# Up-projection jobs over two and four token quarters, a ring of eight value tiles, and softmax denominators as columns

## The reference

```
cq, ckv, kr, z = split(h @ w_in)                       # 384, 256, 32, 1024 columns
q  = rmsnorm(cq, q_norm) @ w_uq                         # 16 heads x (64 nope + 32 rope)
kv = rmsnorm(ckv, kv_norm) @ w_ukv                      # 16 heads x (64 key + 64 value)
q_rope, k_rope = rope(q[..., 64:], pos), rope(kr, pos)
s  = (q_nope @ k_nope.T + q_rope @ k_rope.T) * scale    # causal
o  = softmax(s) @ v
y  = (o * silu(z)) @ w_out
```

## Time and profile before

| | |
|---|---|
| median of 3 runs | 3116.81 us (3113.44 to 3117.73) |
| profiled execution | 3119.66 us |
| its span | 3117.8 us |
| mean granted TensorE clock | 0.977 |
| DMA over the span | 541.14 MB, 173 GB/s |

### The profile page before, as it was taken

The page is one execution under the profiler, slowest core; times in us unless marked ns, Lnnn a source line. Parts: engine busy times, 40 slices in busy tenths (PEclk is TensorE's granted clock), DMA queues, the critical chain, the costliest instruction groups (busy, mean ns, idle before and its releaser), DMA issues. The chain is left out here.

```text
span 3117.8 us, 41010 instructions
## 1 busy us (share of the span) xinstructions
PE 2946.5 (95%) x13537; PEld 2317.2 (74%) x13537; DVE 1909.3 (61%) x2696; ACT 1628.0 (52%) x2830; POOL 1450.3 (47%) x1163
## 2 busy tenths in 40 slices
PE   7999987998999999999987799999999999899998
PEld 6888885666888787778765477777777777588876
DVE  3543315552588765555653587787887877358875
ACT  3111114766445544444544277777777777544543
POOL 0022104764233440000753388888888888523343
PEclk9999998999999999999999699999999999999999
DMA  5233447665996765554999634434435433498674
GB/s 163 84 131 121 118 126 229 190 207 173 301 273 223 237 211 182 171 163 154 325 357 346 160 72 92 109 74 100 101 72 109 92 72 104 120 300 275 224 236 146
DMA packets 294279, 541.14 MB, mean 174 GB/s; under 512 B 29952, under 2 KB 117632, under 8 KB 286912
## 3 DMA queue, kind: packets, MB, share of 16 engines
q1 hardware_dynamic: 219840, 391.23, 42.6%
q10 hardware_dynamic: 74240, 147.49, 15.4%
HBM read 357.86 MB, written 180.49 MB: 173 GB/s over the span
## 5 line engine op out<-in xcount | busy, mean ns | idle before, releaser
L2528 POOL TENSOR_TENSOR mla_pl<-mla_p,mla_ph 128x512 fp32r<-128x512 f32 (+3 forms) x640 | 707.3, 1120 | 164.0 <-ACT mla_p L2388 156.4
L1479 PE MATMUL end_bank<-end_xh,end_whi 128*128 128x512 f32 x1808 | 717.7, 397 | 45.7 <-DVE end_wlo L1710 17.8
L1481 PE MATMUL end_bank<-end_xh,end_wlo 128*128 128x512 f32 x1808 | 708.1, 392 | 0.0
L1480 PE MATMUL end_bank<-end_xl,end_whi 128*128 128x512 f32 x1808 | 707.9, 392 | 0.0
L1548 ACT CAST end_whi<-early_wraw 128x1024 fp32r<-128x1024 f32 (+1 forms) x228 | 234.0, 1027 | 579.7 <-PE end_bank L1481 520.4
L2387 ACT ACTIVATE mla_ph<-mla_score 128x512 fp32r<-128x512 f32 (+3 forms) x640 | 341.3, 533 | 244.8 <-PE mla_score L2230 239.4
L1710 DVE TENSOR_TENSOR end_wlo<-early_wraw,end_whi 128x1024 fp32r<-128x1024 f32 x188 | 258.2, 1374 | 322.6 <-ACT end_whi L1548 322.2
L1479 PEld LDWEIGHTS end_bank<-end_xh,end_whi 128*128 128x128 f32 x1808 | 342.0, 189 | 135.7 <-DVE end_wlo L1710 25.2
L2411 DVE TENSOR_REDUCE mla_mx<-mla_mx 128x1 f32<-128x512 f32 (+3 forms) x640 | 371.8, 604 | 92.6 <-PE mla_mx L2230 91.9
L2461 DVE TENSOR_TENSOR mla_acc<-mla_acc,mla_p 128x512 f32<-128x512 f32 (+3 forms) x576 | 349.1, 606 | 118.3 <-ACT mla_p L2388 114.4
L1480 PEld LDWEIGHTS end_bank<-end_xl,end_whi 128*128 128x128 f32 x1808 | 342.2, 189 | 72.7 <-issue 2.9
(11 more groups left out here) (235 smaller groups left out, 4983.4 us busy)
## 6 DMA issues: line engine op xcount, KB each, us to landing
early_wraw<-in_pe_gate ACTq DMA_DIRECT2D x64, 512.0 KB, 5.1
early_wraw<-in_w_out ACTq DMA_DIRECT2D x62, 512.0 KB, 7.6
early_wraw<-in_w_in ACTq DMA_DIRECT2D x56, 512.0 KB, 3.8
scratch_q<-in_rope SPq DMA_DIRECT2D x64, 256.0 KB, 2.9
swa_q<-scratch_q SPq DMA_DIRECT2D x8, 2048.0 KB, 9.5
end_factor<-scratch_inv SPq DMA_DIRECT2D x64, 256.0 KB, 9.9
scratch_proj<-end_out_f SPq DMA_DIRECT2D x64, 256.0 KB, 6.8
scratch_sum<-end_out_f SPq DMA_DIRECT2D x64, 256.0 KB, 6.2
```

The lines of the kernel that those rows point to most:

```text
L1479: nc.tensor.matmul(bank, wh[:, at], xh[:, k0 + k, :], start=(k == 0), stop=False)
L1480: nc.tensor.matmul(bank, wh[:, at], xl[:, k0 + k, :], start=False, stop=False)
L1481: last = nc.tensor.matmul(bank, wl[:, at], xh[:, k0 + k, :], start=False, stop=(k == kc - 1))
L2528: pool.tensor_tensor(p_lo[b][:, off:TC], prob[b][:, off:TC], p_hi[b][:, off:TC].bitcast(F32), ALU.subtract).then_inc(p_lo_ok, 1)
```

## The change

The four "uq" jobs become two, each of two quarters, and the four "ukv" jobs become one over all four, so that each weight block is loaded, cast and split once for two quarters (uq) and once in all (ukv). In uq the tiles of a block pair run for the first quarter and then for the second; pairs 1 and 4, and 2 and 5, are interleaved, so that both slots are in use together. The slices of a set are ordered k first, then quarter. A weight split is now placed where both the block before has begun and the block before last has ended. Cosine and sine of the second quarter go to the two free slices of the job's raw set. In ukv all key tiles come before all value tiles. Value tiles go to a ring of eight places in both raw sets instead of three. In the attention, `denominator` makes the four times 128 sums the weights and one column of ones the moving side, so that a chunk's denominators land as four columns; ACT copies these into a 128x256 tile, and at the end of the phase two transposes, two copies and one store replace the 64 row stores. The window attention keeps its rows.

```diff
-            jobs += [(stage, q) for stage in ("in", "uq", "ukv") for q in range(NTC)]
+            jobs += [("in", q) for q in range(NTC)] + [("uq", 0), ("uq", 2), ("ukv", 0)]
+        quarters = dict(uq=2, ukv=NTC)
...
-                for pair in (0, 3, 1, 4, 2, 5):
-                    b = new_block(stage, pair, 2, 2 * Q_LORA)
...
+                for mates in ((0,), (3,), (1, 4), (2, 5)):
+                    mine = [new_block(stage, pair, 2, 2 * Q_LORA) for pair in mates]
+                    for t in (q, q + 1):
+                        for b, pair in zip(mine, mates):
+                            tiles += pair_tiles(b, pair, t)
...
-                    tiles += [dict(job=j, kind="split", i=4 * g + i, q=q, block=b, at=i) for i in range(4)]
+                    tiles += [dict(job=j, kind="split", i=4 * g + i, q=t, block=b, at=i)
+                              for t in range(NTC) for i in range(4)]
...
-                    tiles += [dict(job=j, kind="v", i=h, q=q, block=b, at=i) for i in range(4)]
+                    tiles += [dict(job=j, kind="v", i=h, q=t, block=b, at=i) for t in range(NTC) for i in range(4)]
...
-        block_end = [b["at"] for b in blocks[1:]] + [total]
+        for n, x in enumerate(tiles):
+            blocks[x["block"]].setdefault("at", n)
+            blocks[x["block"]]["end"] = n + 1
...
+        split_at = {}
+        for b in range(n_w, len(blocks)):
+            split_at.setdefault(max(blocks[b - 1]["at"], blocks[b - n_w]["end"]), []).append(b)
...
-            turn_cos, turn_sin = square[0], square[1]
+            def tables_of(n):
+                x = tiles[n]
+                spare = raw[x["job"] % 2]
+                return (square[0][:], square[1][:]) if x["q"] % 2 == 0 else (spare[:, 6, :], spare[:, 7, :])
...
+        n_vals = 8
+        v_stored = [s.sem(f"v_stored{b}") for b in range(n_vals)]
...
         def v_tile(n):
-            m = (values[n] - 1) % 3
-            return raw[tiles[n]["job"] % 2][:, 2 + 2 * m:4 + 2 * m, :].rearrange(
+            m = (values[n] - 1) % n_vals
+            mine = raw[(tiles[n]["job"] - (m < n_vals // 2)) % 2]
+            m %= n_vals // 2
+            return mine[:, 2 * m:2 * m + 2, :].rearrange(
...
-            eng.wait_ge(x_lo, pieces_upto[tiles[n]["job"] - 2])
-            if m >= 3:
-                wait_v_stored(eng, v_tiles[m - 3])
+            eng.wait_ge(x_lo, pieces_upto[tiles[n]["job"]])
+            eng.wait_ge(dve_out, by_dve[turn_tiles[-1]])
+            if m >= n_vals:
+                wait_v_stored(eng, v_tiles[m - n_vals])
...
                 if latent and n == total - 4:
-                    for m in range(first[-2], first[-2] + 8):
+                    for m in range(first[-2] + 24, first[-2] + 32):
                         wait_stored(sp, m)
...
+                if nq > 1 and n == first[j]:
+                    pe.wait_ge(x_lo, pieces_upto[j])
...
             def denominator(c):
...
-                mm(o_ps[c % 2][:], consts["ones"][:], acc[c % 2][:], True, True).then_inc(den_ok, 1)
+                for j in range(TC // P):
+                    last = mm(o_ps[c % 2][:, j:j + 1], acc[c % 2][:, j * P:(j + 1) * P], consts["ones"][:, 0:1], True, True)
+                last.then_inc(den_ok, 1)
+
+            def turn_denominators():
+                pe.wait_ge(row_ok, len(chunks))
+                for b in range(n_den // P):
+                    op = nc.tensor.transpose(score[b][:, 0:P], den_cols[:, b * P:(b + 1) * P], consts["ident"][:])
+                op.then_inc(den_turned, 1)
...
+                    per = TC // P
+                    act.copy(den_cols[:, per * c:per * (c + 1)], o_ps[c % 2][:, 0:per]).then_inc(row_ok, 1)
...
+            def store_denominators():
+                act.wait_ge(den_turned, 1)
+                for b in range(n_den // P):
+                    op = act.copy(den_t[:, b, :], score[b][:, 0:P])
+                op.then_inc(den_copied, 1)
+                act.wait_ge(den_copied, 1)
+                act.dma_start(cfg["dens_dst"], den_t[:]).then_inc(dens_stored, 16)
```

More of the change, by code:

```diff
@@ L1071, in chain_phase, with chunks @@
         if latent:
-            jobs += [(stage, q) for stage in ("in", "uq", "ukv") for q in range(NTC)]
+            jobs += [("in", q) for q in range(NTC)] + [("uq", 0), ("uq", 2), ("ukv", 0)]
+        quarters = dict(uq=2, ukv=NTC)
         depth = dict(proj=KD, wo=KD, pe=KD, uq=Q_LORA // P, ukv=KV_LORA // P)
         depth["in"] = KD
+        def chunks(stage):
+            return depth[stage] * quarters.get(stage, 1)
         tiles, first, blocks = [], [], []
         def new_block(stage, i, loads, width):
-            blocks.append(dict(stage=stage, i=i, at=len(tiles), loads=loads, width=width))
+            blocks.append(dict(stage=stage, i=i, loads=loads, width=width))
             return len(blocks) - 1
@@ L1151, in row_ends @@
             return n == mates[0], n == mates[-1]
-        n_pieces = [-(-depth[stage] // 2) for stage, _ in jobs]
+        n_pieces = [-(-chunks(stage) // 2) for stage, _ in jobs]
         pieces = [(j, p) for j in range(len(jobs)) for p in range(n_pieces[j])]
@@ L1164, in part_of, with quarter_of @@
             j, p = pieces[n]
-            return slice(2 * p, min(2 * p + 2, depth[jobs[j][0]]))
+            return slice(2 * p, min(2 * p + 2, chunks(jobs[j][0])))
+        def quarter_of(j, c):
+            stage, q = jobs[j]
+            return q + c % quarters.get(stage, 1)
         def slot_of(j, part):
@@ L1452, in _ @@
                     sp.wait_ge(turn_stored[b], 16 * len(turn_tiles))
[L1453 to L1454 removed]
+                for b in range(n_vals):
+                    sp.wait_ge(v_stored[b], 16 * sum((values[n] - 1) % n_vals == b for n in v_tiles))
         @block.tensor
@@ L1466, in tile @@
                 k0, kc = (2 * x["q"], 2) if kind == "proj" else (0, depth[jobs[j][0]])
+                nq = quarters.get(jobs[j][0], 1)
+                if nq > 1:
+                    k0 = x["q"] - jobs[j][1]
+                if nq > 1 and n == first[j]:
+                    pe.wait_ge(x_lo, pieces_upto[j])
                 wh, wl = w_hi[b % n_w], w_lo[b % n_w]
@@ L1545, in split_w @@
                 if b >= n_w:
-                    act.wait_ge(product, block_end[b - n_w])
+                    act.wait_ge(product, blocks[b - n_w]["end"])
                 width = blocks[b]["width"]
@@ L1676, in _ @@
                 x = tiles[n] if n < total else None
-                if x and x["block"] >= 1 and blocks[x["block"]]["at"] == n and x["block"] + 1 < len(blocks):
-                    if x["block"] + 2 < len(blocks):
-                        load_block(x["block"] + 2)
-                    split_w(x["block"] + 1)
+                if x and x["block"] >= 1 and blocks[x["block"]]["at"] == n and x["block"] + 2 < len(blocks):
+                    load_block(x["block"] + 2)
+                for b in split_at.get(n, []):
+                    split_w(b)
                 if 1 <= n <= total:
@@ L1915, in _ @@
                     evict(n - 1)
-                if x and x["block"] >= 1 and blocks[x["block"]]["at"] == n and x["block"] + 1 < n_dve_blocks:
-                    split_w(x["block"] + 1)
+                for b in split_at.get(n, []):
+                    if b < n_dve_blocks:
+                        split_w(b)
                 if before and before["kind"] != "wo":
@@ L2000, in _ @@
                 x = tiles[n] if n < total else None
-                if x and blocks[x["block"]]["at"] == n and n_dve_blocks <= x["block"] + 1 < len(blocks):
-                    split_w(x["block"] + 1)
+                for b in split_at.get(n, []):
+                    if b >= n_dve_blocks:
+                        split_w(b)
                 if n and tiles[n - 1]["kind"] == "turn" and tiles[n - 1]["at"] == 1:
@@ L2222, in _ @@
                 sp.wait_ge(stored[b], 16 * len(range(b, len(chunks), small)))
-                sp.wait_ge(den_stored[b], 16 * len(range(b, len(chunks), small)))
+                if not long:
+                    sp.wait_ge(den_stored[b], 16 * len(range(b, len(chunks), small)))
+            if long:
+                sp.wait_ge(dens_stored, 16)
             if sinks is not None:
```

102 lines of the change are left out of this document (57 added, 45 removed).

## The result

The changed kernel takes 3082.84 us (median of 4 runs, 3080.85 to 3089.78) against 3115.12 us for the kernel before on the same chip: ratio 0.9891 [0.9877, 0.9906], 32 us less. Run again later (e11_same) it took 3087.65 us, ratio 0.9900 [0.9885, 0.9915]. The forecast was 3077, range 3050 to 3101.

The account below looks back on a forecast made before the run. The prediction took transfers to bound both up-projection stages and TensorE's own work the attention. Its terms, -11.5 (query), -29.7 (key and value) and +1 (attention), sum to -40 us: 3077 us, range 3050 to 3101.

Parts of the forecast that it names:

- Key and value stage: ukv up-projection: transfers stay the bound, 37.2 MB at 360 GB/s in 103.3 us instead of 133, 29.7 us less.
- the bytes' part: ukv stage: 7.9 MB fewer at 339 GB/s are 23 us, called half of the 29.7 us gain.
- rival B: ukv key tiles: the six-tile output ring sets 1.7 us a tile, not bytes; 3095 us; chance 0.20 together with another rival.
- over 112 us: Sign that the output ring rules: ukv stage over 112 us with a DMA share under 0.9.
- eight value tiles that keep the queues filled: ukv stage: eight value tiles instead of three raise the mean rate from 339 to 360 GB/s, the rest of the gain.
- Query stage: uq up-projection: 34.4 MB take 95.6 us, TensorE becomes the bound; with stalls 99.5 us instead of 111, 11.5 us less.
- the rotations' waits and the first ukv tile's: Up-projections: waits for the previous rotation's store and for four activation pieces priced at nothing, 2 us each if uncovered.
- The sentence on the sixth block: uq stage: GpSimd's queue holds a rotation's two sums first, so this weight block can be 0 to 1.5 us late.
- Rival E: uq stays at 111 us, TensorE waiting for interleaved blocks' weights; only ukv gains; 3089 us; chance 0.20 together with another rival.
- Denominators: Attention: eight weight loads 0.117 us apart cost 0.94 us a chunk instead of 0.87, 4.5 us more; copy saves 3.5 to 5.
- C: Attention's one-column pairs are cheap, 0.06 us each: 29 us better than the price taken, 3048 us; chance 0.09.
- D: Attention's one-column pairs don't overlap, 0.41 us each: 154 us more, 3230 us; chance 0.09 with its milder forms.

Follow-up runs that it names:

- e11_same, e11: The changed kernel run again unedited; 3087.65 us, ratio 0.9900 to the kernel before.
- e4: The changed kernel with a ring of four value tiles instead of eight; ratio 0.9919 to the kernel before.
- e7: The changed kernel with only the query jobs merged, key and value jobs one per quarter with a ring of three value tiles; ratio 0.9962 to the kernel before.
- e2: The changed kernel with the attention's denominators as rows, as before the change; ratio 0.9907 to the kernel before.
- e1: The kernel before with only the attention's denominators changed to columns, its up-projection stages unchanged; ratio 0.9991 to the kernel before.

## Why the prediction came out as it did

**Key and value stage, forecast 29.7 us less, measured 31.0: right in the sum, and in part by luck.** The bytes fit: rate times length gives 46.0 MB before and 37.5 after, forecast 37.2, and the mean rate was 359 GB/s, forecast 360. (The prediction calls the bytes' part half of the gain; its own 23 of 29.7 us are three quarters.) But the mean is made of two halves that it did not tell apart. The key tiles took 1.58 us each (32 casts from 1587.1 to 1636.2), between the 1.46 of the bytes and the 1.7 of rival B, and ScalarE waited 21.6 us in them for stores of their low parts: B's ring was at work, though over 112 us did not come. The value tiles took 1.32 us each with TensorE busy 40.4 of 41 us, so there TensorE was the bound, not the transfers. The other part of the reason, eight value tiles that keep the queues filled, was larger than needed: e4 has a stage 2 us longer with four. ScalarE's wait for its own value stores, 24.6 and 14.5 us in the earlier trace rows, is gone in the changed kernel (the value groups from 1640 us):

```profile
L1656 ACT CAST end_raw<-end_bank 128x512 fp32r<-128x512 f32 x16 | 9.4, 587 | 12.4 <-PE end_bank L1517 12.4
L1656 ACT CAST early_raw<-end_bank 128x512 fp32r<-128x512 f32 x12 | 7.0, 587 | 9.3 <-PE end_bank L1517 9.3
```

**Query stage, forecast 11.5 us less (99.5 us), measured 1.1 more: wrong.** Two of its steps failed. The smaller one is the start: the window of 111 us reached 0.8 us before the stage and 2.8 us past its end; cut at events it was 107.4, so 3.6 us of the gain were never there (the stage after was 135.4 and not 133). The larger is the step that put three of the four kv pieces into this stage as 1.6 MB of bytes and nothing else: their preparation has no term (GpSimd is only credited with 12 x 1.93 us less to do, not charged with three more scalings of 2.5 us), and the rotations' waits and the first ukv tile's stand at nothing, with "if that cover is gone, 2 us each". The forecast of 99.5 us describes e7, which doesn't have those pieces: 99.6 us, TensorE at full clock throughout. With them it is 108.5. What the runs show in the step's place is a cost of 9 to 11 us for the four pieces in one stage, at a mean rate of 314 GB/s where the kernel before had 346, so that the bytes alone do not set it; which part of the preparation does is open. The sentence on the sixth block, "0 to 1.5 us late", named the right place: in the changed kernel it was 4 us late, and the half clock after it cost 3 more. Rival E, the query stage unchanged because TensorE waits for a weight part, is what happened there, and its 3089 is near the second measurement, 3087.65; but it blamed the interleaved blocks, and e7 has the same interleaving and no wait over 0.9 us.

**Denominators, forecast 4.5 us more for the products and 3.5 to 5 less for the copy: about right.** The loads stand 0.1125 us apart, forecast 0.117; rivals C (0.06) and D (0.19 or more) are out. That is 0.03 us a chunk more instead of 0.07, and the copy's wait is gone, so a head is 0.26 us shorter, just outside the "within 0.2" I had named. The Trainium skill, "TensorE: Matmul & The Clock Gate", section "LDWEIGHTS (loading the stationary operand)", would have eight loads in 0.85 us by its rate (an estimate); the trace has 0.90, between it and my 0.94. I had written that the cold start is unchanged: it isn't, the clock's return about 10 us later in most profiles takes the 3.9 us back. (The saving of the copy was also summed loosely: 15 times 0.22 us are 3.3, the low end 3.5; TensorE's waits for the copy fell from 7.2 us to 0.3.)

**End of the attention, forecast 1 us more: cannot be told.** From the last head's transpose to the end of the program are 492.2 us before (span 3117.8 less 2625.6), 493.2 and 493.5 in the changed kernel's profiles. But e2, which has rows, has 493.1, and e1, which has columns, 492.3. The rest of the phase alone, from that transpose to the next phase's load of the denominators, is 65.0 and 66.0 us with rows (before, e2) and 65.6, 65.6 and 66.0 with columns (the changed kernel, e11, e1).

**The sum.** Forecast -11.5 - 29.7 + 1 = -40, measured -32. In spans, the changed kernel's second profile against the one before is -32.7: start of the stage -2.7 (variation), query +0.7, key and value -31.2, attention -0.8, end +1.3. So the query term was 12 us off, and the others gave 4 to 5 of that back, of which the 2.7 of the start are luck. The range held the time because I had put that term's failure, E, inside it.

## What to carry to other kernels

Cut a stage at events that both kernels have, not at round times: windows 3.6 us longer than the stage invented a gain of that size. When jobs are merged so that the next job's operands must all be ready at once, their loads and preparation move as a whole into the job before; price them there by each engine's work on them and by what stands behind it in that engine's order, not by their bytes alone: a scaling of 2.5 us ahead of a weight block's subtraction was enough to stop TensorE. And when a merge seems to bring nothing, run each merge alone: the two-by-two table showed in two runs a gain of 8 to 9 us and a cost of 9 to 11 that the combined kernel hid.

## What the runs showed of the hardware that was not expected

A pause of TensorE costs more than itself: after the 3.96 us of the changed kernel the matmuls ran 0.43 us apart for 6 us, half clock. A shorter one was followed by it too: in the kernel before, after a pause of 2.30 us up to 1550.09 the clock was half for 3.4 us. e7's query stage, with no pause over 0.9 us, has PEclk 1.00 throughout.

Eight one-column products cost no less than two products of 512 columns (0.90 and 0.87 us), and the columns went with a later return of the full clock at the attention's start in nine of eleven profiles.

Value tiles with their 512 KB stores moved at a higher rate than the key tiles of the same stage, at nearly the same DMA share (changed kernel; the last two numbers are share and GB/s); why is not shown:

```profile
1587.00:1637.00 50.00, 48.33 (x199) 35.77 (x198) 24.89 (x35) 21.27 (x37) 5.52 (x4) 1.00 1.01 347
1637.00:1678.00 41.00, 40.36 (x179) 33.09 (x177) 21.64 (x32) 18.33 (x32) 1.75 (x1) 1.00 1.03 404
```

So the 360 GB/s that I took as the saturated rate is a mean of two, 347 and 404, and holds only for this mixture.
